# Further passes of an overfull expert in four column tiles of 32 tokens, and the next expert's gate/up weights always ahead of the down weights

## The reference

```python
def moe_ffn(h, router_w, router_b, w_gu, b_gu, w_down, b_down):   # h: (1, 256, 1024) f32
    logits = t @ router_w + router_b                    # 32 experts
    top_val, top_idx = lax.top_k(logits, 4)
    gates = softmax(top_val)
    # for every expert e and the tokens x that chose it:
    gu = x @ w_gu[e] + b_gu[e]                          # (1024, 2048), 8 MB
    g, u = split(gu); g = min(g, 7); u = clip(u, -7, 7)
    y = ((u + 1) * g * sigmoid(1.702 * g)) @ w_down[e] + b_down[e]   # (1024, 1024), 4 MB
    # out[token] += gate * y
```

## Time and profile before

| | |
|---|---|
| median of three runs | 1445.78 us |
| the profiled execution | 1443.56 us |
| its span | 1441.5 us |
| PE busy | 1340.4 us (93%) |
| SP queue's transfers | 476.12 MB, 82.5% of 16 DMA engines |
| weight transfers in the expert loop | 384 of 1 MB |
| DVE, ACT busy | 436.8 us, 228.7 us |

### The profile page before, as it was taken

How to read it: one execution, slowest core, us unless ns; L and a number is a source line. 1 busy time by engine, 2 the same in 40 slices (tenths; PEclk the granted TensorE clock), 3 DMA queues, 4 the chain that set the end, 5 groups by cost and what they waited for, 6 DMA issues and landing times.

```text
span 1441.5 us, 17010 instructions
## 1 busy us (share of the span) xinstructions
PE 1340.4 (93%) x6088; PEld 610.8 (42%) x6089; DVE 436.8 (30%) x909; ACT 228.7 (16%) x411; POOL 15.1 (1%) x47
## 2 busy tenths in 40 slices
PE   4999999999997999999999999999999976799997
PEld 2866865877853333333332233333333322233332
DVE  1001333222223233333333233233333322232433
ACT  3001223776011010010011000010010000000101
POOL 0000000111000000000000000000000000000000
PEclk9999999999996999999999999999999999999999
DMA  9747566312855999999999999999999997479994
GB/s 366 258 136 264 185 232 233 105 72 86 327 216 222 394 415 417 416 419 418 418 417 416 418 418 419 414 418 417 416 419 419 418 417 325 154 310 419 419 418 188
DMA packets 100899, 477.74 MB, mean 331 GB/s; under 512 B 8435, under 2 KB 9020, under 8 KB 65020
## 3 DMA queue, kind: packets, MB, share of 16 engines
q1 hardware_dynamic: 100580, 476.12, 82.5%
q10 hardware_dynamic: 280, 1.05, 0.2%
HBM read 476.09 MB, written 1.05 MB: 331 GB/s over the span
## 4 chain that ended last, share of the span: by engine, by line
PE 79%; DMA 10%; SPq 6%; issue 2%; DVE 1%; ACT 1%; DVEq 0%; ACTq 0%
PE bank L1390 26%; PE bank L1422 12%; PE bank L1138 12%; DMA down_ring<-in_w_down 7%; PE bank L1236 4%; PE bank L1129 4%; PE bank L1349 4%; PE bank L1379 4%; PE bank L1357 3%; SPq L367 3%; SPq L362 2%; PE bank L1297 2%; DMA gu_ring<-in_w_gu 2%; DMA gu_ring<-in_w_ada 1%; PE bank L1083 1%
## 5 line engine op out<-in xcount | busy, mean ns | idle before, releaser
L1390 PE MATMUL bank<-gu_ring,scratch 128*64 128x512 f32 x2048 | 466.2, 602 | 22.2 <-issue 19.8
L1390 PEld LDWEIGHTS bank<-gu_ring,scratch 128*64 128x64 f32 x2048 | 143.9, 138 | 311.9 <-issue 306.3
L1422 PE MATMUL bank<-down_ring,scratch 128*64 128x512 f32 x1024 | 231.0, 597 | 9.9 <-DMA down_ring<-in_w_down 9.9
L1138 PE MATMUL bank<-gu_ring 128*128 128x256 f32 x768 | 173.3, 384 | 2.1 <-ACT gu_ring L528 2.1
L1138 PEld LDWEIGHTS bank<-gu_ring 128*128 128x128 f32 x768 | 145.1, 192 | 27.2 <-issue 7.9
L636 ACT ACTIVATE scratch<-bank 128x512 f32<-128x512 f32 x32 | 19.1, 598 | 739.6 <-PE bank L1390 739.6
L1422 PEld LDWEIGHTS bank<-down_ring,scratch 128*64 128x64 f32 x1024 | 69.0, 136 | 149.0 <-issue 122.0
L969 DVE TENSOR_TENSOR scratch<-bank,bgu 128x512 f32<-128x512 f32 x32 | 22.1, 692 | 280.6 <-PE bank L1357 280.6
L951 DVE TENSOR_TENSOR xres<-xres,bank 128x512 f32<-128x512 f32 x132 | 81.9, 683 | 51.5 <-PE bank L1379 51.5
L1357 PE MATMUL bank<-ident,scratch 128*128 128x128 f32 x400 | 65.8, 288 | 24.6 <-ACT scratch L632 22.7
L1357 PEld LDWEIGHTS bank<-ident,scratch 128*128 128x128 f32 x400 | 42.2, 141 | 106.7 <-ACT scratch L632 51.1
(11 more groups left out here) (249 smaller groups left out, 813.9 us busy)
## 6 DMA issues: line engine op xcount, KB each, us to landing
gu_ring<-in_w_gu SPq DMA_DIRECT2D x256, 1024.0 KB, 20.0
down_ring<-in_w_down SPq DMA_DIRECT2D x128, 1024.0 KB, 16.3
gu_ring<-in_w_in SPq DMA_DIRECT2D x32, 1024.0 KB, 7.9
gu_ring<-in_w_ada SPq DMA_DIRECT2D x20, 1024.0 KB, 8.9
down_ring<-in_w_ada SPq DMA_DIRECT2D x4, 1024.0 KB, 10.3
gu_ring<-in_w_pa SPq DMA_DIRECT2D x4, 1024.0 KB, 6.3
gu_ring<-in_w_pb SPq DMA_DIRECT2D x4, 1024.0 KB, 6.4
gu_ring<-in_w_o SPq DMA_DIRECT2D x4, 1024.0 KB, 10.0
```

The costliest lines, as they stand in the source:

```text
L1138: last = M(dst[:, b * T:(b + 1) * T], group_chunk(group, kt // 4)[:, kt % 4, cols], hT[:, kt, :], start=kt == 0, stop=kt == KT - 1)
L1390: last = M(bank[f // 2][64 * a:64 * a + 64, :], xT[:, kt % 4, kt // 4, :], gu_ring[:, 8 * half + kt, f * 512:(f + 1) * 512], start=kt == 0 ...
L1422: last = M(bank[7][64 * a:64 * a + 64, :], act_sb[:, kt % 4, kt // 4, :], down_ring[:, kt // 2, (kt % 2) * D + a * 512:(kt % 2) * D + (a + ...
```

## The change

A further pass takes 32 tokens (`FCAP`) instead of 64. Four matmuls stand side by side, in PSUM rows 0, 32, 64 and 96: the four column blocks of gate/up all go to bank 0, and down takes its two column blocks times even and odd `kt`. Up to six copies of the pass stand in the code instead of three, for PE, ACT and DVE. In the pass, the tensors of ACT and DVE are half as wide, the transposes are fewer, the way back is transposed earlier, and PE's wait for `y_ready` moves behind gate/up. In SP's queue, gate/up of i+1 stands ahead of down of i for all experts.

```diff
 CAP = 64
-BLOCKS = T // CAP
+FCAP = 32
+FURTHER_BLOCKS = (T - CAP) // FCAP
@@ further_passes
-                for b in range(1, BLOCKS):
+                for b in range(1, FURTHER_BLOCKS + 1):
                     with eng.If(count > b - 1):
@@ block.sync
-            with sp.Fori(1, TOGETHER // 2) as n:
+            with sp.Fori(1, PAIRS - 1) as n:
                 load_item_gu(n * 2 + 1, 1)
                 load_item_down(n * 2)
                 load_item_gu(n * 2 + 2, 0)
                 load_item_down(n * 2 + 1)
-            load_item_down(TOGETHER)
-            load_item_gu(TOGETHER + 1, 1)
-            load_item_down(TOGETHER + 1)
-            with sp.Fori(TOGETHER // 2 + 1, PAIRS) as n:
-                for half in range(2):
-                    load_item_gu(n * 2 + half, half)
-                    load_item_down(n * 2 + half)
+            load_item_gu(NE - 1, 1)
+            load_item_down(NE - 2)
+            load_item_down(NE - 1)
@@ act, further
-                A(g_raw, bank[0][:, :], ACT.Copy)
-                A(u_raw, bank[1][:, :], ACT.Copy).then_inc(f_raw, 1)
+                A(g_raw, bank[0][:, :], ACT.Copy).then_inc(f_raw, 1)
@@ tensor, further
-                pe.wait_ge(y_ready, expert + 1)
                 pe.wait_ge(back_ready, expert + 1)
@@
-                    for a in range(2):
-                        last = M(bank[4][64 * a:64 * a + 64, :], onehot[:, tt, :], xn[:, tt, a * 512:(a + 1) * 512],
+                    for q in range(4):
+                        last = M(bank[4][FCAP * q:FCAP * (q + 1), 0:2 * P], onehot[:, tt, 0:FCAP],
+                                 xn[:, tt, q * 2 * P:(q + 1) * 2 * P], start=tt == 0, stop=tt == TT - 1,
@@
                 for kt in range(KT):
                     for f in range(4):
-                        a = f % 2
-                        last = M(bank[f // 2][64 * a:64 * a + 64, :], f_xT[:, kt % 4, kt // 4, :],
+                        last = M(bank[0][FCAP * f:FCAP * (f + 1), :], f_xT[:, kt % 2, kt // 2, :],
                                  gu_ring[:, 8 * half + kt, f * 512:(f + 1) * 512],
@@
+                pe.wait_ge(y_ready, expert + 1)
                 pe.wait_ge(f_act, k + 1)
                 for kt in range(KT):
                     for a in range(2):
-                        last = M(bank[7][64 * a:64 * a + 64, :], act_sb[:, kt % 4, kt // 4, :],
+                        row = 64 * a + FCAP * (kt % 2)
+                        last = M(bank[7][row:row + FCAP, :], act_sb[:, kt % 4, kt // 4, 0:FCAP],
                                  down_ring[:, kt // 2, (kt % 2) * D + a * 512:(kt % 2) * D + (a + 1) * 512],
```

More of the change, by code:

```diff
@@ L917, in _ @@
             dve.wait_ge(counts_done, 1)
-            for k in range(BLOCKS - 1):
-                own.then(V.tensor_scalar(over[:, k:k + 1], bank[2][0:NE, 0:1], float(CAP * (k + 1)), None, ALU.is_gt))
-            V.tensor_reduce(over[:, 3:4], over[:, 0:3], AX.X, ALU.add).then_inc(over_ready, 1)
+            for k in range(FURTHER_BLOCKS):
+                own.then(V.tensor_scalar(over[:, k:k + 1], bank[2][0:NE, 0:1], float(CAP + FCAP * k), None, ALU.is_gt))
+            V.tensor_reduce(over[:, FURTHER_BLOCKS:FURTHER_BLOCKS + 1], over[:, 0:FURTHER_BLOCKS], AX.X, ALU.add
+                            ).then_inc(over_ready, 1)
             def take(item):
@@ L993, in further, with by_rows @@
                 bias = bgu[:, bass.ds(expert, 1), :].rearrange("p e r -> p (e r)")
-                for tt in range(TT):
[L995 to L1000, removed]
+                def by_rows(t):
+                    return t.rearrange("p (a j) -> p j a", a=2).unsqueeze(3).to_broadcast([P, 4, 2, FCAP])
@@ L1001, in further @@
+                dve.wait_ge(f_onehot, k * 2 + 2)
                 dve.wait_ge(back_ready, expert + 1)
                 for tt in range(TT):
-                    for a in range(2):
[L1004 to L1008, removed]
+                    V.tensor_scalar(gated[:, tt, :, :].rearrange("p a (k s) -> p (a k) s", k=2),
+                                    onehot[:, tt, 0:FCAP].unsqueeze(1).to_broadcast([P, 4, FCAP]),
+                                    gates[:, tt, bass.ds(expert, 1)], None, ALU.mult).then_inc(f_gated, 1)
@@ L1430, in further @@
                 pe.wait_ge(xTe_ready, expert + 1)
[L1431 removed]
                 pe.wait_ge(back_ready, expert + 1)
[L1433 removed]
+                pe.wait_ge(f_onehot, k * 2 + 2)
                 for tt in range(TT):
[L1435 to L1437 removed]
+                    for q in range(4):
+                        last = M(bank[4][FCAP * q:FCAP * (q + 1), 0:2 * P], onehot[:, tt, 0:FCAP],
+                                 xn[:, tt, q * 2 * P:(q + 1) * 2 * P], start=tt == 0, stop=tt == TT - 1,
+                                 skip_group_check=True)
                 last.then_inc(f_taken, 1)
+                pe.wait_ge(f_gated, k * 2 + 2)
+                for tt in range(TT):
+                    last = nc.tensor.transpose(bank[5][:, tt * P:(tt + 1) * P],
+                                               gated[:, tt, :, :].rearrange("p a s -> p (a s)"), ident[:])
+                last.then_inc(f_back_done, 1)
                 pe.wait_ge(f_xraw, k + 1)
[L1440 removed]
+                for c in range(2):
+                    last = nc.tensor.transpose(bank[6][:, c * P:(c + 1) * P], x_raw[:, c * P:(c + 1) * P], ident[:])
+                last.then_inc(f_takenT, 1)
                 pe.wait_ge(f_xT_ready, k + 1)
@@ L1450, in further @@
                 pe.wait_ge(f_raw, k + 1)
-                transposes(2, g_raw)
-                transposes(3, u_raw).then_inc(f_guT_done, 1)
-                pe.wait_ge(f_gated, k + 1)
-                for tt in range(TT):
-                    last = nc.tensor.transpose(bank[5][:, tt * P:(tt + 1) * P],
-                                               gated[:, tt, :, :].rearrange("p a s -> p (a s)"), ident[:])
-                last.then_inc(f_back_done, 1)
+                transposes(2, g_raw).then_inc(f_guT_done, 1)
+                pe.wait_ge(y_ready, expert + 1)
                 pe.wait_ge(f_act, k + 1)
@@ L1484, in _ @@
             pe.wait_ge(over_ready, 1)
-            M(bank[3][0:1, 0:NE], over[:, 3:4], ident[0:NE, 0:NE], start=True, stop=True)
-            M(bank[3][0:1, NE:2 * NE], over[:, 3:4], before[0:NE, 0:NE], start=True, stop=True).then_inc(passes_done, 1)
+            M(bank[3][0:1, 0:NE], over[:, FURTHER_BLOCKS:FURTHER_BLOCKS + 1], ident[0:NE, 0:NE], start=True, stop=True)
+            M(bank[3][0:1, NE:2 * NE], over[:, FURTHER_BLOCKS:FURTHER_BLOCKS + 1], before[0:NE, 0:NE], start=True, stop=True).then_inc(passes_done, 1)
             take_transposed(0)
```

50 lines of the change are left out of this document (26 added, 24 removed).

## The result

The changed kernel takes 1651.14 us (1648.64 to 1660.29) against 1445.39 us (1444.41 to 1447.06): a ratio of 1.142, interval 1.137 to 1.147. The direction was forecast, the size was not: 1466 was predicted, with an upper end of 1474.

The account below looks back on a forecast made before the run. Weights set the pace until 1217 us, and from the pass to the end PE sets the time. The terms 17.0 - 8.6 + 0.6 + 10.5 + 0.9 = +20.4 us on 1445.8 give 1466.2; range 1453 to 1474.

Parts of the forecast that it names:

- Part 3: PE's jumps over the copies behind the pass: four stalls of 3.49 us instead of one, +10.5 us.
- Rival 4: PE's longer loop no longer fits its sequencer and turns stall throughout: some +80 us, about 1530; chance 0.04.
- the three extra thresholds: Tiny DVE operations ahead of the loop that delay PE: 0, at most 0.5 us.
- part 1: Load order, gate/up ahead of down through experts 17 to 24: expert 24 ends later, +17.0 us.
- part 2: The four-tile pass: from expert 24's end to the pass's down end, 29.7 instead of 38.3 us, -8.6 us.
- part 4: Restart of gate/up for expert 25 after longer PE idleness: 5.93 instead of 5.08 us, +0.9 us.
- PE paces the end: From expert 27 on, PE and not transfers sets the time: 27.88 us per expert.
- Rival 2: In the pass, four tiles run no faster than two: +4.4 us, in all 1470.6; chance 0.07.
- Rivals 1: Behind the pass, the jumps cost nothing more: +9.0 us, 1454.8; chance 0.17.
- Rival 3: Experts 17 to 24: the loads' order costs nothing; 1446.2, or 1434.8 without the jumps' cost; chance 0.06.

Follow-up runs that it names:

- dve5: The changed kernel with five copies of the pass in DVE's code instead of six (PE and ACT keep six): 1461.86 us, ratio 1.013.
- before_dve6: The kernel before with six copies of the pass in DVE's code instead of three, left where they fall: 1445.44 us, ratio 1.0005.
- order_only: The kernel before with the new load order alone (64 tokens, two tiles, three copies): 1461.50 us, ratio 1.012.
- nested6: The changed kernel with the copies' conditions nested, so one jump behind the pass instead of five: 1454.48 us, ratio 1.005.
- tiles_old_nested: The changed kernel with the old load order and the copies' conditions nested: 1432.38 us, ratio 0.991.
- slots 0 and 48: The changed kernel, six copies, with DVE's loop placed at slot 0 or 48 of a 256-instruction fetch block: 1462.73 us and 1460.35 us (single run).
- slot 111: The changed kernel with DVE's loop placed at slot 111 of a 256-instruction fetch block: 1585.88 us in a single run.
- before_dve6_placed: The kernel before with six copies in DVE's code and DVE's loop placed at slot 100 of a fetch block: 1588.75 us, ratio 1.099.
- slot 100: The changed kernel with DVE's loop placed at slot 100 of a 256-instruction fetch block: 1462.23 us in a single run.

## Why the prediction was wrong, step by step

**The step that failed is one that it does not have.** Part 3 weighs what six copies do to PE's code and says nothing of DVE's, though the text on the change names PE, ACT and DVE. Rival 4, code that no longer fits and stalls throughout, is the right mechanism on the wrong engine: it looks at PE alone, gives it 0.04, and its argument, "the number of separate pieces that a turn touches is unchanged", is right for PE (q8 has 34 fetches, none of them between 520 and 1360 us, that is from the loop's first turns to the pass) and was never tried on DVE. For DVE the prediction has one term only, the three extra thresholds, at 0 to 0.5 us. Rival 4's price, +80 us, is worked out from two PE stalls per two experts; DVE had five fetches in a turn, some 5 us apart, and they cost 189 us against dve5. The range ended at 1474 with rival 4 left out at 0.04. A count of DVE's instructions from the loop's head to its end would have shown that the loop grows from 187 to 289 instructions, beside fetches of 128, and so that a risk is there. It would not have shown the loss: the loop of 319 instructions in before_dve6 lost nothing where it fell.

**Take that one cause away, and the rest can be compared term by term.** The run dve5 is the changed kernel without it: 1461.86 us measured, 1466.2 predicted; span 1458.9, predicted 1461.9. Its profile is 2.9 us earlier than that of before already when expert 0 is done (482.03 against 484.92), so times on the clock of the run are to be read with 2.9 us added. PE there, from the end of expert 24 to the start of expert 25:

```profile
1185.14 1.94 PE L1422 MATMUL bank<-down_ring,scratch 128*64 128x512 f32 x8 [0.61 <-DMA down_ring<-in_w_down]
1189.86 1.94 PE L1435 MATMUL bank<-xn,onehot 128*32 128x256 f32 x16 [2.78 <-DVE onehot L1001]
...
1193.97 7.07 PE L1452 MATMUL bank<-gu_ring,scratch 128*32 128x512 f32 x64 [0.97 <-DVE scratch L1011]
...
1207.84 1.94 PE L1465 MATMUL bank<-down_ring,scratch 128*32 128x512 f32 x8 [5.43 <-DMA down_ring<-in_w_down]
...
1215.40 1.86 PE L1465 MATMUL bank<-down_ring,scratch 128*32 128x512 f32 x8 [0.51 <-DMA down_ring<-in_w_down]
...
1221.84 0.33 PE L1478 MATMUL bank<-ident 128*128 128x128 f32 x1 [1.68 <-DVE xres L1028]
1238.57 6.51 PE L1390 MATMUL bank<-gu_ring,scratch 128*64 128x512 f32 x16 [16.40 <-issue]
```

| Step | predicted | measured | from |
|---|---|---|---|
| part 1, the order | +17.0 us | +15.7 us; +15.8 and +15.6 from expert 0 to 24 | order_only, whole kernel; order_only and dve5 |
| part 1, expert 24 ends | 1191.3 | 1187.1 | above |
| part 2, gate/up of the pass | 8.7 us | 7.07 us | above; 15.65 before |
| part 2, the pass waits for its own down weights | yes, last lands at 1219.6 | yes, its matmuls start at 1215.4 | above |
| part 2, end of expert 24 to the end of the pass's down | 29.7 us | 1187.1 to 1217.3, 30.2 us | above |
| part 3, PE from the last transpose to expert 25 | 14.5 us | 16.7 us | above; 4.04 before |
| part 4, first 16 parts of gate/up | 5.93 us | 6.51 us | above |
| expert 25 starts | 1241 | 1238.6 (1241.5 with the 2.9) | above |
| PE paces the end | 27.88 us per expert | 27.89 us (1363.91 to 1391.80) | chain of dve5 |

Part 3's four stalls of 3.49 us were five: the first jump, which was to find its target at hand, missed as well. The conditional jumps of the changed kernel, beside the first of the earlier trace rows:

```profile
L331 PEldq COMPARE_BRANCH  x6: 70/3448/3769, 1358.0 to 1409.7; - x6
```

One of the six is the untaken jump ahead of the pass (70 ns), the other five took 3.0 to 3.8 us each. **Rival 2** falls: L1452 takes 7.07 us where two tiles took 15.65, or 13.95 at full clock by the prediction's estimate, so four column tiles do run side by side. The 1.7 us for a slow clock that part 2 added did not come in dve5 (granted clock 1.00 from 1194 to 1201 us); in nested6 the same matmuls took 9.84. The Trainium skill ("TensorEngine Tiling (Array Packing)", Performance Considerations) gives 4x for 32 columns and 2x for 64, and the 7.07 against 13.95 agrees. **Rivals 1 and 3** fall with 16.4 us behind the pass and with order_only. Rival 3's world of loads that cost nothing is not this kernel's, but its arithmetic of a pass whose weights are in time is what tiles_old_nested brings: 1434.8 us without the jumps' cost by the prediction, 1432.38 measured.

**Why the time was above rival 4's too.** In the changed kernel DVE's waits ahead of `gated` total 459.7 us, in dve5 34.3. Of the 425 us between them 189 arrive in the kernel's time; much of the rest lies beside PE's own gate/up matmuls (in the turn shown, from 1180.7 to 1195.8 us, while PE does L1390 until 1196.5) and costs nothing. What is left is 34.5 to 37.8 us per turn ahead of the pass instead of 27.9 to 30.5 in dve5.

## What to carry to other kernels

Code that never runs still has a place: before a change adds copies, unrolled bodies or cases to a loop, count each engine's instructions between the loop's first and last, not only those of the busiest engine, and compare with the size of one instruction fetch. The length alone doesn't decide (319 instructions were fast, 289 slow); the number of fetches on q8 and q14 in the page tells whether a loop refetches. If it does, a loop's place can be worth more than its content: the same instructions took 1589 or 1443 us. And a transfer order that is as good in bytes can cost what stands ahead of a serial section: with gate/up of the next expert first, expert 24 ended 15.6 to 15.8 us later, more than the 11 to 12 us that the four tiles gain in either order. Last, what a faster pass gains can be lost in the jumps behind it: five of them took 16.4 to 21.5 us, one 3.1 to 5.8.

## What the runs showed of the hardware

- All runs fit a DVE sequencer that keeps four pieces of 8 KB and reuses them: where the count gives four pieces per turn q14 has 11 entries in the whole execution (slots 0 and 48), where it gives five it has 167 (slot 111, and before_dve6_placed). The piece behind the one that runs has to be counted among them if DVE stays in its piece for some time; with only five instructions beyond the border it did not count (slot 100: 12 entries). That last rule rests on slots 100 and 111, a single run each.
- The Trainium skill ("Runtime: NRT & Kernel Launch", Instruction fetch mechanics) gives 32 KiB for most engines and 128 KiB for PE. Four pieces of 8 KB agree with the first. It also gives blocks of 16 KiB; q8's fetches are of that size (0.49 MB in 30), q14's are half of it (1.35 MB in 165). The page calls the memory a FIFO with purely sequential prefetch and no cache; the turns from 560 to 1180 us of the kernel before, with no entry on q8 or q14, disagree, and so do the 0.2 us jumps of the earlier trace rows.
- An instruction fetch costs DVE some 5 us while weights stream (stalls of 5.4, 5.0 and 5.0 us in the turn of the changed kernel that is shown, of 5.5 and 6.3 at slot 111; all the idleness ahead of `gated` is 0.90 where nothing is fetched), and PE 3.0 to 3.8 us per jump while the DMA is idle; five jumps with the transfers running in part took 21.5 us instead of 16.4.
- Four f32 matmuls of 32 stationary columns and 512 moving ones side by side take half the time of two pairs of 64: 64 recorded parts in 7.07 us at a granted clock of 1.00, against an estimate of 13.95 us for the pairs at that clock, from the pace of L1390.
